# The scan's inputs u by channel ahead of group in one DMA, and the lag rows in one piece per partition, issued from ScalarE's queue

## The chip, the cores and the metric

One core of one Trainium2 chip runs the whole kernel in one launch. The metric is device time in microseconds, the median of three runs.

## The reference

One encoder layer on x of 2048 positions by 1024 channels, all float32:

```
n = rmsnorm(x);  proj = n @ w_in               # q, k, v and u, 512 columns each
att = diff_attention(q, k, v)                  # 4 heads, ALiBi
ssm = bi_s5_glu(u)                             # 32 groups of 16 channels, 64 complex states, both directions
h = x + [att, ssm] @ w_out
h = h + relu(rmsnorm(h) @ w1)^2 @ w2;  y = rmsnorm(h)
```

`bi_s5_glu` runs a linear recurrence x_t = a x_(t-1) + B u_t over the 2048 positions in each direction, reads out C x_t, adds a skip term d u_t, and gates the gelu of the sum.

## The kernel before

The kernel has four phases: the projection, attention, the scan with its gate (`phase_ssm`), and the output projection with the MLP. The change lies in the scan, with a small part in the projection.

**Layout of the scan.** The 2048 positions are NJ = 256 chunks of T = 8 steps. The 32 groups are worked off in NQU = 4 quarters of G = 8 groups; each group has GH = 16 channels. A step of the loop is one pair (group, direction), so a quarter has 16 steps and the phase NPAIR = 64. `u_t` holds the inputs of two quarters: partition (s, h), that is step in chunk and channel, and free dimensions group and chunk. `load_u` fills it for a quarter with eight DMAs, one for each s, each of 16 partitions by 8 groups in runs of 256 floats (1 KB), since `u_s` in HBM lies as (g h) s j.

**Within a chunk** an output depends on the inputs of the same chunk through a 128 by 128 matrix for each group, `toeplitz`, whose block (s, s') depends on the lag alone. TensorE computes the blocks of the 15 lags (`lags`, line 1923), ScalarE copies them to `strip` (16 partitions; `make_strip`, lines 1712 and 1713), GpSimd adds the two terms of the middle lag (`add_middle`, 1679 and 1681), and eight DMAs on the sync engine's queue (`load_toeplitz`, 1582) copy eight windows of `strip` to eight blocks of 16 partitions of `toeplitz`, in runs of 128 floats (512 B).

**A step on each engine.** TensorE: `inputs(n)`, two matmuls against `u_t` (1936, 1937); at i = 8 to 11 of a quarter four transposes of the next quarter's `bp` (`turn_b`, 1910); at i = 12 and 14 half of the next lags; and at each second step `outputs`, output number m = (step - 6)/2: the matmul with `toeplitz` (1947), then four with `cp` (1952). So the first output of quarter q, number 8q, is in TensorE's order behind step 16q + 6. VectorE: `turn_back` (1806), `add` (1812), `scan` (1820) and for the forward direction `turn_forward` (1567); GpSimd has the backward one. ScalarE: `gelu(m)` (1721), which then issues the store of its result to `z_s` (1723) on its own queue. TensorE may be no more than two steps ahead of `turn_back`, and every engine works in program order.

**The sync engine** issues everything else in a fixed order, group by group (n from 0 to 31): at the first group of a quarter `bp` and `cp` of the next (1358, 1371, 1373), at the second `load_u` of the next, at the seventh `load_toeplitz` of the next; for each group the table six groups ahead (`load_tab`, 512 KB, once both directions of group n are through) and the load of z of three groups back (`load_z`, once its store has landed). `load_toeplitz(0)` stands ahead of the loop and waits for GpSimd. At step 32 VectorE also splits the gate's weights (1851).

**Projection.** `split_w(i)` splits the i-th piece of 128 columns of `w_in` in a high and a low part on ScalarE (644) and VectorE (734); pieces 12 to 15 are those of u. `evacuate_qku` writes their results (759) and `store` stores them to `u_s` (547).

Of the kernel before, what the change touches and what calls it, by code (L numbers as in the profile page):

```python
# [17 lines left out]
F32 = mybir.dt.float32  # L18
# [375 lines left out]
def phase_project(nc, ctx, shared, x_t, norm1_g, w_in, qk_s, v_s, u_s, prep_in, attention_in):  # L394
# [110 lines left out]

    @block.sync
    def _(sp):
# [25 lines left out]
        def store(n):  # L533
# [197 lines left out]
    def _(dve):  # L731
        def split_w(i):
            dve.wait_ge(w_hi_ready, i + 1)
            dve.tensor_tensor(w_lo[:, :, w_slot(i)], w_raw[:, i % 2], w_hi[:, :, w_slot(i)].bitcast(F32),  # L734
# [602 lines left out]
class SsmHead:  # L1337
# [88 lines left out]
def phase_ssm(nc, ctx, place, shared, head, following, mag, s_d, w_glu, b_glu, z_s, ssm_s, att_s, att_square, att_floor,  # L1426
# [22 lines left out]
    strip = place.sb("sm_strip", 4096, [GH, G, 2 * T - 1, GH])  # L1449
# [4 lines left out]
    toeplitz = place.sb("sm_toeplitz", 38912, [P, 2, G, P])  # L1454
# [115 lines left out]
    def _(sp):  # L1570
# [6 lines left out]
        def load_toeplitz(q):  # L1577
            sp.wait_ge(strip_step, 4 * q + 4)
            if q >= 2:
                sp.wait_ge(y_done, (q - 1) * G)  # L1580
            for s in range(T):
                sp.dma_start(toeplitz[s * GH:(s + 1) * GH, q % 2].rearrange("p g (s h) -> p g s h", s=T),
                             strip[:, :, T - 1 - s:2 * T - 1 - s]).then_inc(toeplitz_loaded, 16)

# [13 lines left out]
        load_toeplitz(0)  # L1598
        for n in range(NGR):
            q, g = n // G, n % G  # L1600
            if q + 1 < NQU:
# [7 lines left out]
                if g == G - 2:  # L1609
                    load_toeplitz(q + 1)  # L1610
# [48 lines left out]
    def _(pool):  # L1659
# [14 lines left out]
        def add_middle(n):  # L1674
            q, half = n // 2, n % 2
            gs = slice(half * 4, half * 4 + 4)
            mid = strip[:, gs, T - 1]
# [16 lines left out]
    def _(act):  # L1694
# [10 lines left out]
        def make_strip(q, half):  # L1705
            n = 2 * q + half
            gs = slice(half * 4, half * 4 + 4)
            fwd, bwd = (lag_ps[0:GH, d].rearrange("p (g s h) -> p g s h", g=4, s=T) for d in range(2))
# [42 lines left out]
        for half in range(2):  # L1751
            make_strip(0, half)
# [1205 lines left out]
```

## Time and profile before

| | |
|---|---|
| median of 3 runs | 2610.61 us (2609.18 to 2612.34) |
| the profiled execution | 2613.55 us, its span 2611.6 us |
| TensorE, VectorE, ScalarE, GpSimd busy | 97%, 80%, 54%, 10% of the span |
| projection and attention | 0 to 958 us |
| scan, first transpose to last output | 959 to 1143.5 us |
| gate | 1143.5 to 1193 us |
| output projection and MLP | from 1193 us |

In a timeline a row has the start, the busy time, the engine and line, the operation and its tiles, the number merged, and in brackets the idle time before it and what ended it. In busy time by stretch, a row has the stretch and its length, then for each engine the busy time and number of instructions, then the granted clock (1.00 is 2.4 GHz, 0.50 is 1.2 GHz), the DMA share (mean busy share of the 16 DMA engines; it can exceed 1 where two queues' packets overlap) and GB/s. PEld is TensorE's weight load, SPq and ACTq are the queues of the sync engine and of ScalarE.

### The profile page before, as it was taken

How to read it: one execution, taken by the hardware profiler on the slowest of the kernel's cores; microseconds unless marked ns; L12 is line 12 of the kernel's file. 1: busy time of each engine (PE TensorE's matmuls, PEld its weight loads, DVE VectorE, ACT ScalarE, POOL GpSimd, SP SyncE). 2: the span in 40 equal slices, each digit the busy share in tenths (PEclk: the TensorE clock that was granted, in tenths of full speed). 3: DMA queues.
4: the chain of work that ended last, by engine and by line, in shares of the span. 5: the costliest groups of instructions: out<-in, count | busy, mean ns of one | idle time of the engine just before them, and what ended most of it. 6: DMA issues, size and time to landing. Idle time of an engine off the chain costs nothing.

```text
span 2611.6 us, 32904 instructions
## 1 busy us (share of the span) xinstructions
PE 2539.0 (97%) x12816; PEld 2077.5 (80%) x12816; DVE 2076.9 (80%) x2116; ACT 1416.9 (54%) x1754; POOL 269.7 (10%) x290
## 2 busy tenths in 40 slices
PE   9998999999999989899989999999999999999998
PEld 7887878878777867778767888888887888888886
DVE  5875759999999967879899777687789877678885
ACT  5276637778787752144435566533345666543334
POOL 3500022212121113310000000000000000000003
PEclk9999999999999999999999999999999999999999
DMA  6256642020204119946485543533334554452221
GB/s 213 111 189 230 235 123 64 25 72 23 72 25 104 32 60 265 265 164 221 182 313 216 210 181 136 224 145 129 123 114 162 220 220 177 177 195 97 97 79 65
DMA packets 158170, 388.78 MB, mean 149 GB/s; under 512 B 29120, under 2 KB 86720, under 8 KB 130240
## 3 DMA queue, kind: packets, MB, share of 16 engines
q1 hardware_dynamic: 142464, 319.58, 37.4%
q10 hardware_dynamic: 15552, 67.12, 6.5%
q8 instruction: 101, 1.65, 0.3%
q14 instruction: 53, 0.43, 0.1%
HBM read 266.58 MB, written 117.96 MB: 147 GB/s over the span
## 4 chain that ended last, share of the span: by engine, by line
PE 51%; DVE 4%; DMA 1%; issue 1%; ACT 0%; POOL 0%; SPq 0%; DVEq 0%; ACTq 0%; POOLq 0%
PE sm_banks L2799 16%; PE sm_banks L2801 16%; PE sm_banks L2800 16%; PE sm_banks L1997 1%; PE sm_banks L1995 1%; PE sm_banks L1996 1%; DVE ml_res L2657 1%; DMA kp_low<-hn_s 0%; DVE ml_b_split L2588 0%; DVE ml_w_split L2599 0%; DVE kp_tabs L2696 0%; DVE ml_hb L2704 0%; DVE ml_rinv L2683 0%; DVE ml_res L2677 0%; PE sm_banks L1952 0%
## 5 line engine op out<-in xcount | busy, mean ns | idle before, releaser
L2799 PE MATMUL sm_banks<-ml_b_split,ml_w_split 128*128 128x512 f32 x2016 | 788.8, 391 | 12.8 <-issue 10.7
L2800 PE MATMUL sm_banks<-ml_b_split,ml_w_split 128*128 128x512 f32 x2016 | 785.8, 390 | 0.0
L2801 PE MATMUL sm_banks<-ml_b_split,ml_w_split 128*128 128x512 f32 x2016 | 785.5, 390 | 0.0
L2799 PEld LDWEIGHTS sm_banks<-ml_b_split,ml_w_split 128*128 128x128 f32 x2016 | 379.6, 188 | 96.9 <-issue 15.6
L2800 PEld LDWEIGHTS sm_banks<-ml_b_split,ml_w_split 128*128 128x128 f32 x2016 | 379.7, 188 | 79.3 <-issue 1.0
L2801 PEld LDWEIGHTS sm_banks<-ml_b_split,ml_w_split 128*128 128x128 f32 x2016 | 379.4, 188 | 79.2
L1082 ACT ACTIVATE at_e<-at_e,at_neg_top 128x2048 f32<-128x2048 f32 x128 | 256.5, 2004 | 143.1 <-DVE at_neg_top L1136 143.1
L2425 ACT ACTIVATE ml_b_split<-kp_u_t 128x2048 fp32r<-128x2048 f32 x54 | 103.6, 1918 | 300.0 <-PE sm_banks L2801 296.4
L2657 DVE TENSOR_TENSOR ml_res<-sm_banks,ml_res 128x2048 f32<-128x2048 f32 x75 | 171.7, 2289 | 114.5 <-PE sm_banks L2801 114.5
L1238 PEld LDWEIGHTS pj_banks<-at_v,at_a_t 128*128 128x128 f32 x2048 | 238.4, 192 | 22.8 <-issue 22.6
L1238 PE MATMUL pj_banks<-at_v,at_a_t 128*128 128x128 f32 x2048 | 255.8, 278 | 0.0
L2588 DVE TENSOR_TENSOR ml_b_split<-kp_low,ml_b_split 128x2048 fp32r<-128x2048 f32 x53 | 121.3, 2288 | 96.5 <-ACT ml_b_split L2425 96.5
L1129 DVE CUSTOM_DVE_ANT_0 at_e<-pj_banks,at_bias,at_top 128x1024 f32<-128x1024 f32 x128 | 164.4, 1284 | 28.0 <-PE pj_banks L1210 25.5
L2425 ACT ACTIVATE ml_b_split<-kp_low 128x2048 fp32r<-128x2048 f32 x53 | 101.5, 1914 | 141.3 <-PE sm_banks L2801 136.0
L2396 POOL TENSOR_TENSOR kp_tabs<-kp_tabs,ml_square 128x512 f32<-128x512 f32 x13 | 22.8, 1750 | 1431.0 <-ACT ml_square L2491 1428.8
L1152 DVE SCALAR_TENSOR_TENSOR at_e<-at_e,at_coef 128x1024 f32<-128x1024 f32 x128 | 164.6, 1287 | 2.3
L1129 DVE CUSTOM_DVE_ANT_0 at_e<-pj_banks,at_bias 128x1024 f32<-128x1024 f32 x128 | 151.6, 1222 | 16.9 <-issue 15.4
L2588 DVE TENSOR_TENSOR ml_b_split<-kp_u_t,ml_b_split 128x2048 fp32r<-128x2048 f32 x54 | 123.4, 2286 | 52.3 <-ACT ml_b_split L2425 52.3
L858 PE MATMUL pj_banks<-pj_x_hi,pj_w_hi 128*128 128x512 f32 x384 | 152.5, 397 | 4.5 <-DVE pj_w_lo L734 4.5
L1205 PE MATMUL pj_banks<-at_k_hi,at_q_hl 128*128 128x512 f32 x512 | 151.7, 416 | 2.6 <-DVE at_top L1129 2.3
L859 PE MATMUL pj_banks<-pj_x_lo,pj_w_hi 128*128 128x512 f32 x384 | 150.3, 392 | 0.0
L860 PE MATMUL pj_banks<-pj_x_hi,pj_w_lo 128*128 128x512 f32 x384 | 150.2, 391 | 0.0
(246 smaller groups left out, 3994.5 us busy)
## 6 DMA issues: line engine op xcount, KB each, us to landing
act_s<-ml_res ACTq DMA_DIRECT2D x32, 1024.0 KB, 3.9
kp_wide<-in_w_stream SPq DMA_DIRECT2D x18, 1024.0 KB, 5.1
kp_tabs<-in_w_stream SPq DMA_DIRECT2D x18, 1024.0 KB, 7.1
kp_bp<-in_w_stream SPq DMA_DIRECT2D x18, 1024.0 KB, 5.5
ml_r<-in_w_stream SPq DMA_DIRECT2D x18, 1024.0 KB, 7.1
tab_s<-kp_tabs ACTq DMA_DIRECT2D x32, 512.0 KB, 2.8
kp_low<-hn_s SPq DMA_DIRECT2D x16, 1024.0 KB, 5.4
kp_u_t<-hn_s SPq DMA_DIRECT2D x16, 1024.0 KB, 4.9
```

Source lines behind the costliest of these rows:

```text
L858: pe.matmul(out, w_hi[:, k, cols], x_hi[:, k], start=(k == 0), stop=False)
L1082: act.activation(self.e[:, n % 2, c], self.e[:, n % 2, c], ACT.Exp, bias=self.neg_top[:, n % 2, c:c + 1], scale=self.SCALE, accum_out=self ...
L1129: dve.tensor_tensor_reduce(out=self.e[:, s % 2, c, half * self.HALF:(half + 1) * self.HALF], in0=self.score[:, c], in1=self.bias[:, at:at ...
L1152: dve.scalar_tensor_tensor(self.e[:, slot, 0, cols], self.e[:, slot, 1, cols], self.coef[:, 1:2], self.e[:, slot, 0, cols], ALU.mult, ALU. ...
L1205: pe.matmul(self.score[:, c, bank * TB:(bank + 1) * TB], self.q_hl[:, n % 2, c], self.k_hi[h % 2][:, c, keys], start=True, stop=False)
L1238: last = pe.matmul(self.pv[:, n % 2, 0:P], self.a_t[:, n % 2, kt], self.v[h % 2][kt], start=(kt == 0), stop=(kt == self.NQ - 1))
L2425: act.activation(b_split[g % 2][:, 0], raw_b(k, i)[:], ACT.Copy).then_inc(b_hi_ready, 1)
L2588: dve.tensor_tensor(b_split[g % 2][:, 1], raw_b(k, i)[:], b_split[g % 2][:, 0].bitcast(F32), ALU.subtract)\
L2657: dve.tensor_tensor(flat(res[reg]), flat(bank(k, i)), flat(res[reg]), ALU.add).then_inc(dve_left, 1)
L2799: pe.matmul(out, w_hi[:, w], b_hi[:, b], start=fresh and kt == 0, stop=False, skip_group_check=True)
L2800: pe.matmul(out, w_hi[:, w], b_lo[:, b], start=False, stop=False, skip_group_check=True)
L2801: last = pe.matmul(out, w_lo[:, w], b_hi[:, b], start=False, stop=kt == 3, skip_group_check=True)
```

## The change

`u_s` is laid out as [quarter, s, channel, chunk], and the channel dimension runs as (h g) where it ran as (g h). For that, the columns of the last four pieces of `w_in` are permuted while they are split: both splits read the raw piece with a stride of 16 floats and write in order. A quarter of u is then one DMA of 128 rows of 8 KB. `strip` is [16, lag, h, g], so that a window of eight lags is one run of 1024 floats (4 KB) per partition, and `toeplitz` holds the group as its last dimension; the matmul reads its weights with a stride of 8 floats (32 B). ScalarE's and GpSimd's writes to `strip` go in runs of four floats. The eight toeplitz DMAs go from the sync engine's program to ScalarE's: for quarter 0 behind `make_strip`, for the others in two halves, behind the gelu of step 16q and of step 16q + 2, that is behind gelu(8q - 3) and gelu(8q - 2).

```diff
     def load_u(self, sp, q):
-        for s in range(T):
-            sp.dma_start(self.u_t[s * GH:(s + 1) * GH, q % 2],
-                         self.u_s[q].rearrange("(g h) s j -> s h g j", g=G)[s]).then_inc(self.u_loaded, 16)
+        sp.dma_start(self.u_t[:, q % 2].rearrange("p g j -> p (g j)"),
+                     self.u_s[q].rearrange("s (h g) j -> (s h) (g j)", g=G)).then_inc(self.u_loaded, 16)
...
-    strip = place.sb("sm_strip", 4096, [GH, G, 2 * T - 1, GH])
+    strip = place.sb("sm_strip", 4096, [GH, 2 * T - 1, GH, G])
-    toeplitz = place.sb("sm_toeplitz", 38912, [P, 2, G, P])
+    toeplitz = place.sb("sm_toeplitz", 38912, [P, 2, P, G])
...
-        load_toeplitz(0)
         for n in range(NGR):
-                if g == G - 2:
-                    load_toeplitz(q + 1)
...
+        def load_toeplitz(q, first, end):
+            act.wait_ge(strip_step, 4 * q + 4)
+            if q >= 2:
+                act.wait_ge(y_done, (q - 1) * G)
+            for s in range(first, end):
+                act.dma_start(toeplitz[s * GH:(s + 1) * GH, q % 2].rearrange("p k g -> p (k g)"),
+                              strip[:, T - 1 - s:2 * T - 1 - s].rearrange("p s h g -> p (s h g)")).then_inc(toeplitz_loaded, 16)
...
+        load_toeplitz(0, 0, T)
         for step in range(NPAIR):
             if output_at(step) is not None:
                 gelu(output_at(step))
+            if q and i in (0, 2):
+                load_toeplitz(q, i * 2, i * 2 + 4)
...
-            pe.matmul(o, toeplitz[:, q % 2, g], u_t[:, q % 2, g], start=True, stop=False)
+            pe.matmul(o, toeplitz[:, q % 2, :, g], u_t[:, q % 2, g], start=True, stop=False)
...
-    u_s = scratch("u_s", [NQU, P, T, NJ])
+    u_s = scratch("u_s", [NQU, T, P, NJ])
```

## Rows read from the trace of the kernel before

**Rows 1.** Busy time by stretch, cut where the first output of a quarter starts

```profile
core 0: us, PE busy (x) PEld busy (x) DVE busy (x) ACT busy (x) POOL busy (x), PEclk, DMA share, GB/s
...
977.40:1017.70 40.30, 37.19 (x192) 31.59 (x193) 34.73 (x61) 10.71 (x23) 15.62 (x13) 1.00 1.07 273
1017.70:1065.80 48.10, 42.34 (x192) 34.90 (x193) 32.90 (x53) 8.79 (x22) 13.06 (x12) 0.89 1.04 262
1065.80:1109.40 43.60, 37.72 (x193) 31.23 (x192) 36.71 (x65) 8.56 (x22) 15.94 (x13) 0.96 1.07 264
1109.40:1143.50 34.10, 31.10 (x133) 25.98 (x134) 29.91 (x47) 7.23 (x14) 10.83 (x10) 0.89 0.49 136
```

**Rows 2.** Timeline of TensorE, 955 to 1146 us: pieces with idle time before them

```profile
977.47 0.67 PE L1947 MATMUL sm_banks<-kp_u_t,sm_toeplitz 128*128 128x256 f32 x2 [0.92 <-DMA sm_toeplitz<-sm_strip]
...
1017.72 1.19 PE L1947 MATMUL sm_banks<-kp_u_t,sm_toeplitz 128*128 128x256 f32 x2 [3.05 <-DMA sm_toeplitz<-sm_strip]
...
1026.51 0.66 PE L1910 MATMUL sm_banks<-sm_ident,kp_bp 128*128 128x128 f32 x4 [3.06 <-DMA kp_bp<-bp_s]
...
1055.64 1.22 PE L1936 MATMUL sm_banks<-kp_u_t,sm_p_t 128*128 128x256 f32 x2 [2.69 <-DVE sm_turned_w L1806]
...
1091.17 0.67 PE L1936 MATMUL sm_banks<-kp_u_t,sm_p_t 128*128 128x256 f32 x2 [0.78 <-DVE sm_turned_w L1806]
...
1109.42 1.19 PE L1947 MATMUL sm_banks<-kp_u_t,sm_toeplitz 128*128 128x256 f32 x2 [4.69 <-DMA sm_toeplitz<-sm_strip]
```

**Rows 3.** Timeline of VectorE, 1046 to 1116 us

```profile
1047.98 0.69 DVE L1806 TENSOR_TENSOR sm_turned_w<-sm_banks,kp_tabs 128x512 f32<-128x512 f32 x1 [2.72 <-DMA kp_tabs<-tab_s]
...
1051.62 3.36 DVE L1851 TENSOR_TENSOR sm_wg_lo<-sm_wg,sm_wg_hi 128x2048 fp32r<-128x2048 f32 x1
...
1114.56 0.69 DVE L1806 TENSOR_TENSOR sm_turned_w<-sm_banks,kp_tabs 128x512 f32<-128x512 f32 x1 [4.19 <-PE sm_banks L1937]
```

**Rows 4.** Timeline of the sync engine's queue, 955 to 1146 us: its DMA issues, merged

```profile
969.92 5.54 SPq L1582 DMA_DIRECT2D sm_toeplitz<-sm_strip  x8
...
1001.41 6.55 SPq L1582 DMA_DIRECT2D sm_toeplitz<-sm_strip  x8
...
1014.29 0.41 SPq L1358 DMA_DIRECT2D kp_bp<-bp_s  x1
...
1017.50 14.37 SPq L1362 DMA_DIRECT2D kp_u_t<-u_s  x8
...
1060.74 0.38 SPq L1358 DMA_DIRECT2D kp_bp<-bp_s  x1
```

**Rows 5.** Timeline of ScalarE: the issue of the seventh z store

```profile
1010.05 0.33 ACTq L1723 DMA_DIRECT2D z_s<-sm_z_g  x1
```

**Rows 6.** DMA issues, 955 to 1146 us: KB each, median us to landing

```profile
z_s<-sm_z_g ACTq DMA_DIRECT2D x32, 128.0 KB, 8.3
...
sm_toeplitz<-sm_strip SPq DMA_DIRECT2D x32, 64.0 KB, 9.3
```

**Rows 7.** The same view of 1117 to 1126 us, where DMA is lighter

```profile
z_s<-sm_z_g ACTq DMA_DIRECT2D x2, 128.0 KB, 3.9
```

**Rows 8.** Busy time in short stretches (columns as in rows 1)

```profile
971.00:977.00 6.00, 4.19 (x16) 2.41 (x14) 5.95 (x11) 0.00 (x0) 1.63 (x1) 1.00 0.62 97
979.50:984.00 4.50, 4.50 (x24) 3.98 (x23) 4.50 (x8) 1.26 (x3) 2.02 (x2) 1.00 1.07 395
992.50:996.50 4.00, 4.00 (x22) 3.36 (x20) 1.89 (x4) 1.50 (x4) 1.31 (x3) 1.00 1.14 136
1018.00:1021.40 3.40, 3.40 (x10) 2.72 (x10) 0.92 (x2) 0.00 (x0) 0.04 (x1) 0.56 1.10 254
```

**Rows 9.** Lines 1947, 756 and 759: ns min/median/max of one

```profile
L1947 PEld LDWEIGHTS sm_banks<-kp_u_t,sm_toeplitz x64: 186/190/337, 977.4 to 1140.8; 128*128 128x128 f32 x64
...
L756 DVE TENSOR_TENSOR pj_qku_out<-pj_banks,kp_bp x32: 681/692/694, 40.1 to 197.3; 128x512 f32<-128x512 f32 x32
...
L759 DVE TENSOR_TENSOR pj_qku_out<-pj_banks,kp_bp x16: 1078/1132/1147, 234.2 to 384.2; 128x512 f32<-128x512 f32 x16
```

More of the change, by code:

```diff
@@ L504, in w_slot, with w_raw_columns, w_split_columns @@
         return slice((i % HALF_W) * P, (i % HALF_W + 1) * P)
+    def w_raw_columns(i):
+        raw = w_raw[:, i % 2]
+        return raw if i < HALF_W + NV else raw.rearrange("p k (g h) -> p k h g", g=G)
+    def w_split_columns(w, i):
+        part = w[:, :, w_slot(i)]
+        return part if i < HALF_W + NV else part.rearrange("p k (h g) -> p k h g", g=G)
     @block.sync
@@ L733, in split_w @@
             dve.wait_ge(w_hi_ready, i + 1)
-            dve.tensor_tensor(w_lo[:, :, w_slot(i)], w_raw[:, i % 2], w_hi[:, :, w_slot(i)].bitcast(F32),
+            dve.tensor_tensor(w_split_columns(w_lo, i), w_raw_columns(i), w_split_columns(w_hi, i).bitcast(F32),
                               ALU.subtract).then_inc(w_lo_ready, 1)
@@ L1575, in load_cp @@
             head.load_cp(sp, q)
[L1577 to L1583, printed above, removed]
         def load_z(n):
@@ L1676, in add_middle @@
             gs = slice(half * 4, half * 4 + 4)
-            mid = strip[:, gs, T - 1]
+            mid = strip[:, T - 1, :, gs].rearrange("p h g -> p g h")
             pool.wait_ge(strip_copied, 3 * n + 3)
@@ L1707, in make_strip @@
             gs = slice(half * 4, half * 4 + 4)
-            fwd, bwd = (lag_ps[0:GH, d].rearrange("p (g s h) -> p g s h", g=4, s=T) for d in range(2))
+            fwd, bwd = (lag_ps[0:GH, d].rearrange("p (g s h) -> p s h g", g=4, s=T) for d in range(2))
             act.wait_ge(lag_done, n + 1)
             wait(act, toeplitz_loaded, 16 * T * q)
-            act.activation(strip[:, gs, T - 1:], fwd, ACT.Copy).then_inc(strip_copied, 1)
-            act.activation(strip[:, gs, 0:T - 1], bwd[:, :, 0:T - 1], ACT.Copy).then_inc(strip_copied, 1)
+            act.activation(strip[:, T - 1:, :, gs], fwd, ACT.Copy).then_inc(strip_copied, 1)
+            act.activation(strip[:, 0:T - 1, :, gs], bwd[:, 0:T - 1], ACT.Copy).then_inc(strip_copied, 1)
             wait(act, strip_step, 2 * n - 1)
-            act.activation(middle[:], bwd[:, :, T - 1], ACT.Copy).then_inc(strip_copied, 1)
+            act.activation(middle[:].rearrange("p g h -> p h g"), bwd[:, T - 1], ACT.Copy).then_inc(strip_copied, 1)
+        def load_toeplitz(q, first, end):
[5 more added lines that the diff above has]
+                              strip[:, T - 1 - s:2 * T - 1 - s].rearrange("p s h g -> p (s h g)")).then_inc(toeplitz_loaded, 16)
         def gelu(n):
```

7 lines of the change are left out of this document (4 added, 3 removed).

## The prediction

> **What bounds the kernel now.** I read first the page, by which TensorE is busy nearly throughout, then the busy time by stretch of the scan, cut at the first outputs (numbers 0, 8, 16, 24) of its four quarters. In the first, 40.3 us long, TensorE has 37.2 us of work at full clock, VectorE 34.7; the second takes 48.1 us and the third 43.6 for the same TensorE work, and the DMA share is over 1 in all three [rows 1]. So a quarter is worth 37.2 us to TensorE, and what lies above is stalls: 3.1, 10.9 and 6.4 us. The DMA engines are full, but only what TensorE waits for counts.
>
> The timeline of TensorE names the stalls: toeplitz not landed (0.92, 3.05, 4.69 us), `bp` not landed (3.06), VectorE late (2.69, 0.78) [rows 2]. Behind the 3.05 comes a stretch of 3.4 us at a granted clock near 0.5 [rows 8], the lower level of 1.2 GHz; it costs half its length, 1.65 us. The mean clock of 0.89 over 48.1 us [rows 1] is 5.3 us lost, or three such stretches, one for each long stall of that quarter (3.05, 3.06, 2.69).
>
> VectorE's timeline says what a stall is worth. The 2.69 stands behind the 3.36 us split of the gate's weights; VectorE had lost 2.72 us to a table a little earlier, but TensorE had not finished the next inputs much earlier: VectorE would have been at the split only about half a microsecond sooner, so without that wait most of the 2.69 remains. The 4.69 became 4.19 us of idle VectorE, which is not idle again by a TensorE stall up to the last scan [rows 3]: 4.2 us is its worth, clock included.
>
> The sync queue's timeline shows who is late: the toeplitz issues hold it 5.54 and 6.55 us, the next `bp` comes behind them, and eight issues of u take 14.37 us [rows 4].
>
> **What the change can give back**, in us of the profiled execution:
>
> - the toeplitz stalls: 0.9, then 3.05 + 1.65 of clock, then 4.2: 9.8
> - the `bp` stall: 3.06 + 1.65 = 4.7. `bp` was issued at 1014.29 and wanted at 1023.45 (1026.51 less 3.06) [rows 2, 4]. The 6.55 us of toeplitz issues no longer stand ahead of it, so it is issued 4 or 5 us sooner, behind less traffic. I count all of it.
> - the late tables: 0.5 of the 2.69 and the 0.78: 1.3
>
> Together 15.8.
>
> **u in one DMA.** While u lands the rate is 136 GB/s at a share of 1.14; with tables, `bp` and `cp` it is 395 at 1.07 [rows 8]. A quarter's 1.05 MB goes from 7.7 us of full engines to 2.7, and the sync queue's eight issues (14.37 us at worst) to one like that of `bp`, 0.53 or less [rows 4]. This is 5 of 40 us of DMA, and it makes the items above likely; it enters the sum only through them. Quarter 0's is loaded in attention, beside other work. The store of u has the same pieces of 256 B and is hidden in the projection: nothing.
>
> **Toeplitz by ScalarE.** What is removed from the sync queue is counted. What is added is the question when the last rows land. ScalarE issues at 0.33 us each, by the z store [rows 5], against some 0.6 to 2.5 on the sync queue; four hold it 1.3 us, and the next gelu is due only an output later, nine matmuls of 0.43 or 3.9 us: free. Even at 0.7 each it would be.
>
> The last four stand behind gelu(8q - 2) and its z store. In quarter 1 that store was issued at 1010.05, and TensorE asked for output 8 at 1014.67 (1017.72 less 3.05) [rows 2, 5]: 4.6 us. At quarter 0, with nothing beside them, the copies ran at 97 GB/s and a share of 0.62 [rows 8], though issues every 0.7 us may have set that. If 97 is the pace, 0.26 MB take 2.7 us; with 0.33 for the store's issue and about 1.8 us of latency (my estimate, from a z store in the light stretch at 3.9 us, less its own transfer and queue) the last rows land 4.8 us behind the z store's issue: a stall of 0.2 at best. At worst they land like a z store under load, 8.3 us behind an issue [rows 6], the last of which is 1.3 us late: 9.6, a stall of 5.0. `bp(q + 1)` is issued at just that time (1060.74 in quarter 2) [rows 4], so neither end is right; the burst of the quarter before has drained, and the z store in the lighter stretch took 3.9 [rows 7]. I take 2.0 for quarters 1 and 2, with half the price of a slow stretch (0.8), since stalls of 0.92 and 2.69 lie on either side of it: 2.8 each. Quarter 3 loads no `bp`, `cp` or u: 1.0.
>
> In quarter 0 the sync queue no longer waits for GpSimd and sends `bp` and `cp` (3.4 MB, 8.6 us at 395 GB/s) at about 968 instead of 975.5, just ahead of the toeplitz rows. Output 0 is asked for at 976.55. Eight issues end at 972.7 instead of 975.5, but at 97 GB/s they land at 977.2 alone and by about 982 behind the whole burst: a stall of 0.7 to 5; I take 2.0 and 0.8 of clock. The writes to `strip` in runs of four floats could add up to 1.2 us, at the ratio below, on this chain alone; that is within the bound. Later strips are copied a third of a quarter ahead.
>
> Toeplitz stalls after: 3 x 2.8 + 1.0 = 9.4.
>
> **The strided weights.** Of 64 weight loads of 190 ns each [rows 9] every one reads 128 floats with a stride of 32 B. They hide behind a matmul pass of 215 ns (two passes of a matmul of 256 columns are 0.43 apart in TensorE's steady state). No TensorE operand in this trace has such a stride. The nearest row is VectorE's line 759, the same tensor_tensor as line 756 but with operands read at a stride of 32 B: 1132 against 692 ns, 0.86 ns more for each of 512 elements [rows 9]. At that price a load takes 300 ns, 85 beyond the pass, and 64 of them 5.4 us. The other end is nothing, and a gain is excluded, as the hidden load can't get under the pass. Since line 759 also reads PSUM so, I take the middle, 2.7.
>
> On this the Trainium skill (SBUF — State Buffer, Door 1, the note on lines of 16 bytes) says that reads which go to a new line each time pay a penalty, so that four fp32 is as far as one strides free. Line 759 agrees; by that rule alone the 5.4 would stand in the sum.
>
> **The split of u's weights** reads with a stride of 64 B, four pieces on each of two engines: at most 0.9 us each, several groups ahead of TensorE's use. Nothing; without that cover, 3.5 us.
>
> **The sum.** 15.8 - 9.4 - 2.7 = 3.7 us. The profiled execution took 2613.55 us (span 2611.6); 2609.9 after. It lies 2.9 above the median shown, so the median becomes 2606.9. From the terms' ends near their values the forecast's own range is 2602 to 2611. A change of less than 0.2% (5.2 us) is about what a measurement of this kernel can't tell from none.
>
> **The rivals.**
>
> 1. *The relief is full.* The toeplitz rows land on time but for 0.7 to 1 us a quarter, and the weights cost nothing: 15.8 - 4 = 11.8, so 2598.8. For it: ScalarE's queue is short, the copies of 4 KB runs may be quicker than 97 GB/s. Against it: `bp` in the same microseconds.
> 2. *The strided weights set the pace.* At VectorE's price in full the gain is 15.8 - 9.4 - 5.4 = 1.0: 2609.6. At twice the load time (380 ns, 165 beyond the pass) it is a loss of 4.2: 2614.8. It would show as a longer TensorE quarter without stalls.
> 3. *The lag rows come later than before: slower.* The sync queue issued those of quarter 1 from 1001.41 to 1007.96 [rows 4], and ScalarE ends them about 3.5 us later; they land like a z store under load. Stalls: 5.0 + 1.65 in quarters 1 and 2, 5.0 in 3, about 5.1 in 0: 23.4 against 15.8 with free weights, so 7.6 slower, 2618. It decides from some 3 us a quarter. The rate is a reason for it: 16 source partitions may allow no more than the 97 GB/s seen, however long the runs.
> 4. *The change doesn't relieve anything that TensorE waits for*, the `bp` stall moving with the toeplitz one: 2610.6.
>
> The Trainium skill (SBUF — State Buffer, Door 1) ties a DMA's rate to how many of 16 ports its partitions reach, and 16 partitions in a row reach four. The 97 GB/s of rows 8 agrees, and it makes rival 3 likelier; u's eight DMAs were of that kind, so for u it speaks for the change.
>
> **Chances.** The forecast 0.38 (0.12 of it beyond 5.2 us faster, 0.26 within); rival 1 0.28; rival 2 0.10, half within and half slower; rival 3 0.17; rival 4 0.07. So faster 0.12 + 0.28 = 0.40, same 0.26 + 0.05 + 0.07 = 0.38, slower 0.05 + 0.17 = 0.22. The range runs from beyond the full relief (2595) to rival 3 (2618).
>
> **What the profile after would show.** u's issues one a quarter; the wait for `bp` at output 8 gone; the 2.69 still there behind line 1851; weight loads of line 1947 between 190 and 300 ns; waits for toeplitz of 1 to 3 us in each quarter, longest in 0 to 2; a DMA share near 0.95. The prediction is wrong if these waits are gone (faster) or over 3 us (slower), or if a stretch of a quarter without stalls is longer than 37.2 us.

## The result and the profile after

| | before | after |
|---|---|---|
| median | 2610.14 us (2609.18 to 2612.34) | 2636.86 us (2635.80 to 2638.40) |
| ratio | | 1.0089 [1.0077, 1.0101], slower |
| span of the profiled execution | 2611.6 us | 2634.6 us |
| scan's first inputs start | 967.9 | 971.3 |
| output 0, 8, 16, 24 start | 977.5, 1017.7, 1065.8, 1109.4 | 988.4, 1038.2, 1085.7, 1130.8 |

The forecast was 2606.9 us and its range ended at 2618. The change is slower by 23 us by the spans of the two profiled executions and by 27 by the medians. Where they come in, in the spans: 3.4 before the scan starts, 7.5 up to output 0, 9.6 in quarter 0 (49.8 us where it had 40.3), then -0.6, +1.5 and +0.3 in quarters 1 to 3, and 1.3 behind the scan.

Busy time by stretch of the kernel after, cut at the same outputs as [rows 1]:

```profile
core 0: us, PE busy (x) PEld busy (x) DVE busy (x) ACT busy (x) POOL busy (x), PEclk, DMA share, GB/s
971.20:988.40 17.20, 7.37 (x31) 4.89 (x29) 11.55 (x20) 2.45 (x4) 3.96 (x4) 0.86 0.95 269
988.40:1038.20 49.80, 40.61 (x192) 34.44 (x192) 33.46 (x56) 10.70 (x23) 14.55 (x12) 0.88 0.68 212
1038.20:1085.70 47.50, 41.56 (x193) 34.95 (x193) 36.35 (x57) 8.91 (x22) 14.53 (x12) 0.93 0.78 215
1085.70:1130.80 45.10, 39.71 (x193) 33.86 (x193) 34.88 (x59) 8.91 (x22) 14.53 (x12) 0.96 0.98 270
1130.80:1165.20 34.40, 31.63 (x131) 27.22 (x132) 30.09 (x46) 7.22 (x14) 10.97 (x10) 0.86 0.29 83
```

The DMA share is down from 1.07, 1.04 and 1.07 to 0.68, 0.78 and 0.98: u no longer fills the engines, as foreseen. The stretches are longer all the same. TensorE's timeline, pieces with idle time before them (it answers to [rows 2]):

```profile
988.36 1.22 PE L1957 MATMUL sm_banks<-kp_u_t,sm_toeplitz 128*128 128x256 f32 x2 [8.46 <-DMA sm_toeplitz<-sm_strip]
...
1038.25 1.22 PE L1957 MATMUL sm_banks<-kp_u_t,sm_toeplitz 128*128 128x256 f32 x2 [9.24 <-DMA sm_toeplitz<-sm_strip]
...
1071.38 0.70 PE L1946 MATMUL sm_banks<-kp_u_t,sm_p_t 128*128 128x256 f32 x2 [2.24 <-DVE sm_turned_w L1816]
...
1085.68 1.07 PE L1957 MATMUL sm_banks<-kp_u_t,sm_toeplitz 128*128 128x256 f32 x2 [3.65 <-DMA sm_toeplitz<-sm_strip]
...
1130.78 1.22 PE L1957 MATMUL sm_banks<-kp_u_t,sm_toeplitz 128*128 128x256 f32 x2 [5.39 <-DMA sm_toeplitz<-sm_strip]
```

The wait for `bp` is gone, though `bp` was not issued sooner: it left 36.5 us behind the start of output 0 (1024.84 less 988.36), before the change 36.8, and the 9.24 us for the lag rows now cover its landing. The 2.69 behind the split of the gate's weights is 2.24. And the waits for the lag rows are 8.46, 9.24, 3.65 and 5.39 us, 26.7 in all, where they were 0.92, 3.05, 0 and 4.69. Behind each of the four, TensorE works for a while at a granted clock of 0.50, the lower level:

```profile
988.40:993.80 5.40, 5.40 (x13) 4.30 (x14) 0.00 (x0) 0.38 (x1) 0.00 (x0) 0.50 0.64 262
1038.30:1041.60 3.30, 3.30 (x8) 2.70 (x9) 0.00 (x0) 0.00 (x0) 0.00 (x0) 0.50 1.00 225
1086.10:1089.40 3.30, 3.30 (x9) 2.64 (x9) 0.00 (x0) 0.00 (x0) 0.00 (x0) 0.50 1.09 317
1130.80:1133.70 2.90, 2.90 (x7) 2.37 (x8) 0.50 (x1) 0.00 (x0) 0.00 (x0) 0.50 1.04 275
```

These are 14.9 us of work that would take half as long at the upper level: 7.4 us lost.

The issues, first on the sync queue (answering to [rows 4]), then on ScalarE's (with [rows 5]):

```profile
971.35 0.32 SPq L1369 DMA_DIRECT2D kp_bp<-bp_s  x1
...
979.72 0.44 SPq L1372 DMA_DIRECT2D kp_u_t<-u_s  x1
...
1024.84 0.62 SPq L1369 DMA_DIRECT2D kp_bp<-bp_s  x1
...
1117.09 0.41 SPq L1594 DMA_DIRECT2D kp_bp<-att_s  x1
...
973.40 5.09 ACTq L1722 DMA_DIRECT2D sm_toeplitz<-sm_strip  x8
...
1024.94 0.33 ACTq L1730 DMA_DIRECT2D z_s<-sm_z_g  x1
1025.32 2.52 ACTq L1722 DMA_DIRECT2D sm_toeplitz<-sm_strip  x4
...
1077.26 2.45 ACTq L1722 DMA_DIRECT2D sm_toeplitz<-sm_strip  x4
...
1120.61 2.46 ACTq L1722 DMA_DIRECT2D sm_toeplitz<-sm_strip  x4
```

u is one issue of 0.44 us. The eight copies of quarter 0 are issued right behind `bp` and `cp` and take ScalarE 5.09 us, 0.63 each and not 0.33. In quarter 1, the second four leave at 1025.32 to 1027.84, `bp` at 1024.84; TensorE asks for the rows at 1029.01 (1038.25 less 9.24) and has them 10.4 us behind the last issue. In quarter 3 the sync queue has a load that the prediction left out: 1 MB of attention's result (line 1594, into the tile of `bp`, which is free by then), issued at 1117.09, 3.5 us ahead of the last four copies. Landings, as in [rows 6]:

```profile
kp_tabs<-tab_s SPq DMA_DIRECT2D x15, 512.0 KB, 5.0
...
z_s<-sm_z_g ACTq DMA_DIRECT2D x32, 128.0 KB, 4.7
...
sm_toeplitz<-sm_strip ACTq DMA_DIRECT2D x32, 64.0 KB, 7.1
```

A z store lands in 4.7 us where it took 8.3. The copies of 4 KB runs on the emptier engines take 7.1 where those of 512 B took 9.3. Line 1957, the matmul with the strided weights, and its load (as [rows 9]):

```profile
L1957 PEld LDWEIGHTS sm_banks<-kp_u_t,sm_toeplitz x64: 312/333/342, 988.3 to 1162.1; 128*128 128x128 f32 x64
L1957 PE MATMUL sm_banks<-kp_u_t,sm_toeplitz x64: 397/403/791, 988.4 to 1162.5; 128*128 128x256 f32 x64
```

The load takes 333 ns for 190, the matmul 403 for 379. And the 3.4 us ahead of the scan are lost in one place, where TensorE waits for the split of a block of x. TensorE's timeline of before, then of after:

```profile
244.83 0.77 PE L853 MATMUL pj_banks<-pj_w_hi,pj_x_hi 128*128 128x512 f32 x1 [8.21 <-DVE pj_x_lo L741]
```

```profile
247.83 0.77 PE L864 MATMUL pj_banks<-pj_w_hi,pj_x_hi 128*128 128x512 f32 x1 [11.29 <-DVE pj_x_lo L752]
```

The first of the four splits of u's weight pieces in the kernel after, its high part on ScalarE and its low part on VectorE (the other three are alike; pieces of other columns take 1.06 and 1.22 us):

```profile
183.64 2.01 ACT L655 ACTIVATE pj_w_hi<-kp_wide 128x1024 fp32r<-128x1024 f32 x1 [2.75 <-DMA kp_wide<-in_w_in]
...
185.68 1.98 DVE L745 TENSOR_TENSOR pj_w_lo<-kp_wide,pj_w_hi 128x1024 fp32r<-128x1024 f32 x1 [2.81 <-ACT pj_w_hi L655]
```

### The profile page after: what moved, and what is told of

Its sections match the earlier page's. It is cut to its first block, busy times and chain, and to the rows that moved or that the text cites. A ratio compares the mean times of both kernels' runs of the same rounds, so it can differ in the third digit from the quotient of the medians.

```text
span 2634.6 us, 32878 instructions
## 1 busy us (share of the span) xinstructions
PE 2545.7 (97%) x12816; PEld 2085.4 (79%) x12816; DVE 2082.2 (79%) x2116; ACT 1420.7 (54%) x1754; POOL 271.1 (10%) x290
## 4 chain that ended last, share of the span: by engine, by line
PE 50%; DVE 4%; DMA 1%; issue 1%; ACT 0%; POOL 0%; SPq 0%; DVEq 0%; ACTq 0%; POOLq 0%
PE sm_banks L2809 16%; PE sm_banks L2811 16%; PE sm_banks L2810 16%; PE sm_banks L2007 1%; PE sm_banks L2005 1%; PE sm_banks L2006 1%; DVE ml_res L2667 1%; DMA kp_low<-hn_s 0%; DVE ml_b_split L2598 0%; DVE ml_w_split L2609 0%; DVE kp_tabs L2706 0%; DVE ml_hb L2714 0%; DVE ml_rinv L2693 0%; PE sm_banks L1962 0%; DVE ml_res L2687 0%
## 5 line engine op out<-in xcount | busy, mean ns | idle before, releaser
L2809 PE MATMUL sm_banks<-ml_b_split,ml_w_split 128*128 128x512 f32 x2016 | 788.9, 391 | 12.6 <-issue 10.4
```

Source lines behind the costliest of these rows:

```text
L2809: pe.matmul(out, w_hi[:, w], b_hi[:, b], start=fresh and kt == 0, stop=False, skip_group_check=True)
```

## The experiments

All were timed in three sets, each beside the kernel before, and ratios are to it, with their 95% intervals. Its median was 2614.66 us in the first set (the four kernels with parts of the change), 2612.73 in the second (`early_issue`, `bp_behind`, `sp_contig`, `sp_write_strided`) and 2614.05 in the third (`sp_late`, `early_bp`, `sp_plain_split`, `sp_outer_later`). So times of different sets are compared by their ratios; a difference of two ratios is taken times 2610 us, and one below 0.15% can't be told from none.

### Which part costs: four kernels with parts of the change

**`u_alone`** has u's layout, its one DMA and the permuted columns; the lag rows are as before.

> Only u's part of the change: the layout of u_s, the permuted split of its weights, one DMA a quarter. The queue theory (what was lost comes from when and where the toeplitz copies are issued): nothing of the 23 us is here, and the relief that the prediction counted on is: the wait for bp at output 8 gone, 3 to 10 us faster than before, 2600 to 2607. The projection theory (the stride-16 reads of the split delay the projection by the 3.4 us by which the first inputs of the scan start later after the change): the scan starts 3.4 us later again and the sum is 0 to 3 us slower, 2610 to 2613.

Measured: 2607.60 us, 0.9973 [0.9963, 0.9983]. The waits for the lag rows fall to one of 0.87 us, with the old 512 B layout, because they land in 3.8 us (9.3 before):

```profile
984.07 0.75 PE L1955 MATMUL sm_banks<-kp_u_t,sm_toeplitz 128*128 128x256 f32 x2 [0.87 <-DMA sm_toeplitz<-sm_strip]
...
sm_toeplitz<-sm_strip SPq DMA_DIRECT2D x32, 64.0 KB, 3.8
```

Both theories hold in part: the relief came, 7 us by the ratio, and the scan starts at 974.5, 6.6 us later than before, with a wait of 13.69 us for the split of x.

**`layout_alone`** has the new `strip` and `toeplitz`, issued by the sync engine as before; u in eight DMAs.

> Only the layout of the lag rows (strip by lag, h, g; toeplitz with the group last; strided weights), copied from the sync engine's queue at the old places; u as before. The queue theory: toeplitz waits stay near those of before (0.9, 3.1, 0, 4.7 us), weight loads of 333 ns cost 0.05 to 0.14 us an output, 2 to 5 us in all: 2612 to 2615. The layout theory (copies in runs of 4 KB are themselves slower and later, weights cost most of the loss): 12 to 20 us slower, 2622 to 2630.

Measured: 2609.87 us, 0.9984 [0.9975, 0.9992]. Waits of 0.65, 1.80 and 3.92 us are left of 0.92, 3.05 and 4.69. Neither theory foresaw a gain; the new layout is a small one by itself, 0.16%, strided weights included.

**`queue_alone`** has the old layouts, and only `load_toeplitz` moved to ScalarE.

> Only the move: the eight copies of a quarter in the old layout (512 B runs) issued by ScalarE at the places of the change. The queue theory: the long toeplitz waits of the changed kernel appear again (8.5 at output 0, 9 at output 8, 4 to 5 at the others), 15 to 20 us slower than before: 2625 to 2630. The layout theory: waits within 2 us of those of before, at most 3 us slower: 2610 to 2613.

Measured: 2654.58 us, 1.0151 [1.0137, 1.0164], worse than the whole change and far beyond the 2625 to 2630 of the queue theory. The waits for the lag rows are 16.20, 16.61, 13.36 and 9.13 us; TensorE's timeline at the first, then the copies of quarter 0 alone:

```profile
991.86 1.19 PE L1947 MATMUL sm_banks<-kp_u_t,sm_toeplitz 128*128 128x256 f32 x2 [16.20 <-DMA sm_toeplitz<-sm_strip]
...
sm_toeplitz<-sm_strip ACTq DMA_DIRECT2D x8, 64.0 KB, 11.2
```

**`after_sp`** is the whole change but for the queue: the sync engine issues the rows at the old places.

```diff
+        load_toeplitz(0)
...
+                if g == G - 2:
+                    load_toeplitz(q + 1)
...
-        load_toeplitz(0, 0, T)
...
-            if q and i in (0, 2):
-                load_toeplitz(q, i * 2, i * 2 + 4)
```

> The whole change but the move: one DMA for u and the new lag layout, toeplitz copies by the sync engine at the old places. The queue theory: the waits at outputs 0 and 8 fall back under 2 us, 2602 to 2612, that is 25 to 35 us under the changed kernel. The layout theory: it stays within 8 us of the changed kernel, 2628 to 2637.

Measured: 2606.74 us, 0.9970 [0.9959, 0.9980]. Only 0.47 and 0.56 us of waits for the rows are left:

```profile
979.54 0.82 PE L1955 MATMUL sm_banks<-kp_u_t,sm_toeplitz 128*128 128x256 f32 x2 [0.47 <-DMA sm_toeplitz<-sm_strip]
...
1097.58 0.82 PE L1955 MATMUL sm_banks<-kp_u_t,sm_toeplitz 128*128 128x256 f32 x2 [0.56 <-DMA sm_toeplitz<-sm_strip]
...
sm_toeplitz<-sm_strip SPq DMA_DIRECT2D x32, 64.0 KB, 5.8
```

So the move to ScalarE's program costs 1.0089 less 0.9970, 1.2% or 31 us, and all else together gains 0.3%. That is the queue theory.

### Late, or in the wrong company?

Two things changed with the move: the rows of quarters 1 to 3 are issued later (quarter 1's from 1020.25 to 1027.84, of a scan that started 3.4 us later, against 1001.41 to 1007.96), and they run beside the sync queue's large loads (`bp` and `cp`, in quarter 3 the 1 MB of attention's result) and not ahead of them.

**`early_issue`**, on the kernel after, issues them one step before the quarter:

```diff
-            if q and i in (0, 2):
-                load_toeplitz(q, i * 2, i * 2 + 4)
+            if q + 1 < NQU and i == 15:
+                load_toeplitz(q + 1, 0, T)
```

> The kernel after, with all eight copies of a quarter's lag rows issued by ScalarE at step 15 of the quarter before (behind the last turned copy and the strip) and not four at step 0 and four at step 2 of the quarter itself. In the kernel after the rows landed 9.24, 3.65 and 5.39 us too late in quarters 1 to 3. Theory A (they are late because they are issued late): the first four now leave about 2 us sooner and the last four about 6 to 7 us sooner, so the waits of quarters 1 to 3 fall from 18.3 us in all to under 4, and the time falls by 12 to 17 us, to a ratio of about 1.003. Theory B (they are late because bp, cp and u, issued at the start of a quarter, share the DMA engines with them): the rows gain only what is moved before the burst starts; the waits fall to some 9 to 12 us, the time by 5 to 8 us, ratio about 1.006. The wait of quarter 0, 8.46 us, is the same by both.

Measured: 2616.77 us, 1.0017 [1.0008, 1.0027], 19 us faster than the kernel after. The waits of quarters 1 and 2 are gone and quarter 3's is 0.32; that of quarter 0 is as it was:

```profile
989.69 1.22 PE L1957 MATMUL sm_banks<-kp_u_t,sm_toeplitz 128*128 128x256 f32 x2 [8.52 <-DMA sm_toeplitz<-sm_strip]
```

Theory A, beyond its own estimate: a few microseconds sooner are enough for quarters 1 to 3. They are not enough to tell company from lateness, since the earlier rows also run ahead of `bp`.

**`bp_behind`**, on the kernel after, holds `bp` and `cp` back until the rows have landed:

```diff
                 if g == 0:
+                    sp.wait_ge(toeplitz_loaded, 16 * T * (q + 1))
                     sp.wait_ge(lag_done, 2 * q + 2)
```

> The kernel after, with one wait more on the sync engine: bp and cp of the next quarter are issued only when this quarter's lag rows have landed. Theory B (the rows share the engines with bp and cp): the eight copies of quarter 0 land as in a quiet stretch, about 3 to 4 us behind the last issue at 978.5 instead of 986.8, so the wait of 8.46 falls to 3 or 4 us, and the others from 9.24, 3.65 and 5.39 to 2 to 4 us each; together 10 to 15 us faster than the kernel after. What it may cost is a late bp, cp or table (up to 3 us). Theory A (they are late because ScalarE issues them late and slowly, 0.63 us each): the waits stay within 1 us of what they were, and the time is that of the kernel after or longer, ratio 1.009 or more.

Measured: 2618.84 us, 1.0027 [1.0013, 1.0040], 16 us faster than the kernel after. TensorE's waits, with the rows issued by ScalarE as in the kernel after, at the same distance from TensorE's need:

```profile
979.90 0.82 PE L1958 MATMUL sm_banks<-kp_u_t,sm_toeplitz 128*128 128x256 f32 x2 [0.52 <-DMA sm_toeplitz<-sm_strip]
...
1020.76 0.82 PE L1958 MATMUL sm_banks<-kp_u_t,sm_toeplitz 128*128 128x256 f32 x2 [2.17 <-DMA sm_toeplitz<-sm_strip]
...
1066.34 0.82 PE L1958 MATMUL sm_banks<-kp_u_t,sm_toeplitz 128*128 128x256 f32 x2 [1.89 <-DMA sm_toeplitz<-sm_strip]
...
1110.60 1.21 PE L1958 MATMUL sm_banks<-kp_u_t,sm_toeplitz 128*128 128x256 f32 x2 [5.57 <-DMA sm_toeplitz<-sm_strip]
```

Landing of the eight copies of quarter 0, here and in the kernel after:

```profile
sm_toeplitz<-sm_strip ACTq DMA_DIRECT2D x8, 64.0 KB, 2.4
```

```profile
sm_toeplitz<-sm_strip ACTq DMA_DIRECT2D x8, 64.0 KB, 8.6
```

Theory B, and again more than it asked: 2.4 us for 8.6, and a wait of 0.52 for 8.46. The packets of the trace show the company. In the kernel after, the 128 packets of 4 KB of quarter 0's rows start between 977.2 and 986.8 us, and 223 packets of the sync queue start between them, 179 of `cp` and 44 of a table (those of `bp` started from 972.3 to 975.5, so the first of the rows started 3.8 us behind its issue); in four equal parts of that time it is 36, 30, 28 and 33 of the rows beside 63, 47, 49 and 64 of the others. With `bp` behind, no other starts between them and they start 1.2 us behind their issue and are through in 4.9 us, which is the pace of ScalarE's issues (eight by 0.63 us). In `queue_alone` the same bytes are 1024 packets of 512 B, and they take 17.0 us beside 1110 others.

Quarter 3 keeps its wait. It isn't a later issue that sets it apart: in quarters 2 and 3 of both kernels the last issue ends 2.3 us before TensorE asks. With that same lead `bp_behind` waits 1.89 us in quarter 2, where its copies land in 4.8 us (median), and 5.57 in quarter 3, where they land in 7.8. What stands beside them there, and `bp_behind` does not hold back, is the 1 MB of attention's result, issued 3.5 us ahead of the last four as in the kernel after. No run holds back that load alone, so its share is argued and not shown.

On this the Trainium skill (DMA: Bandwidth & Descriptors, Queues, rings and completion order) says that a DMA engine takes the queues in turn and works off a whole packet of some 9 to 17 descriptors of one before it goes to the next. That would fit with small copies that wait for several rows of `cp` each time. The rows of the trace don't say which engine moved them, so the length of a turn isn't shown here.

**`sp_late`** tells the two apart the other way round: the sync engine's queue, with `bp` behind the rows, but in quarters 1 to 3 issued at the start of the quarter. Against `after_sp`:

```diff
+            if q and g == 0:
+                load_toeplitz(q)
             if q + 1 < NQU:
                 if g == 0:
...
-                if g == G - 2:
-                    load_toeplitz(q + 1)
```

> The kernel of the run after_sp, but the sync engine issues the lag rows of quarters 1 to 3 only at the start of the quarter itself, just ahead of bp and cp, at about the time at which ScalarE does in the kernel after. Theory A (the time of issue decides): they come too late as in the kernel after, by about 3 to 8 us in each of quarters 1 to 3, a ratio of 1.004 to 1.008. Theory B (ScalarE's queue decides, because its packets take turns with those of the sync engine's queue while bp and cp stand behind the rows on the sync engine's own): the waits are 1 to 3 us each as in bp_behind, 0.52, 2.17 and 1.89 there in the first three quarters, and the ratio is 1.000 or less.

Measured: 2622.86 us, 1.0036 [1.0022, 1.0049].

```profile
1021.24 1.22 PE L1955 MATMUL sm_banks<-kp_u_t,sm_toeplitz 128*128 128x256 f32 x2 [3.68 <-DMA sm_toeplitz<-sm_strip]
...
1068.44 1.22 PE L1955 MATMUL sm_banks<-kp_u_t,sm_toeplitz 128*128 128x256 f32 x2 [4.18 <-DMA sm_toeplitz<-sm_strip]
...
1114.33 1.22 PE L1955 MATMUL sm_banks<-kp_u_t,sm_toeplitz 128*128 128x256 f32 x2 [5.10 <-DMA sm_toeplitz<-sm_strip]
...
sm_toeplitz<-sm_strip SPq DMA_DIRECT2D x32, 64.0 KB, 3.5
```

Each copy lands in 3.5 us, the quickest of all these kernels, and still they come 3.7 to 5.1 us too late. But they were issued later than was meant: in quarters 1 to 3 the last issue ends 1.8, 2.0 and 1.2 us behind TensorE's asking (1017.56 in quarter 1), where in the kernel after it ends 1.2, 2.3 and 2.3 us ahead of it. So these waits show what lateness can do and are not its share in the kernel after. Theory A is nearer, but neither is whole: late issue costs 0.66% over `after_sp` (17 us), and the kernel after another 0.53% (14 us), by its waits in quarters 0 and 1 (8.46 and 9.24 us, here 0.46 and 3.68), where its rows run beside `cp`, in quarter 1 beside `bp` too.

**`early_bp`** puts both remedies on the kernel after: `early_issue`, and `bp` behind the rows in quarter 0 alone.

> The kernel of the run early_issue (ScalarE issues a quarter's eight copies at step 15 of the quarter before; 1.0017 of before), and in quarter 0 alone the sync engine holds bp and cp back until the lag rows have landed, as in bp_behind, where the wait of quarter 0 was 0.52 us instead of 8.5. If the loss of the change is made of these two things, issued late in quarters 1 to 3 and behind bp and cp in quarter 0, both together take it away: waits for the lag rows of under 2 us in all, 7 to 9 us faster than early_issue, ratio about 0.9985 to 0.997, that of after_sp. If ScalarE's queue costs something of its own beside that, the ratio stays over 1.000.

Measured: 2607.07 us, 0.9979 [0.9969, 0.9989], where `after_sp` has 0.9970. Waits of 0.56 and 0.32 us for the rows are left (and in quarter 1 of 1.76 for `bp` and 1.44 for `cp`):

```profile
980.80 0.82 PE L1959 MATMUL sm_banks<-kp_u_t,sm_toeplitz 128*128 128x256 f32 x2 [0.56 <-DMA sm_toeplitz<-sm_strip]
...
1103.07 0.82 PE L1959 MATMUL sm_banks<-kp_u_t,sm_toeplitz 128*128 128x256 f32 x2 [0.32 <-DMA sm_toeplitz<-sm_strip]
```

ScalarE's queue by itself costs nothing that these runs can tell. The time of issue and the large loads beside it are the whole loss. They overlap: in quarter 1 either remedy alone takes most of the wait away (9.24 us to 0 by issuing earlier, to 2.17 by holding `bp` back).

### The strides

**`sp_contig`**, on top of `after_sp`:

```diff
-            pe.matmul(o, toeplitz[:, q % 2, :, g], u_t[:, q % 2, g], start=True, stop=False)
+            pe.matmul(o, toeplitz[:, q % 2].rearrange("p k g -> p (k g)")[:, g * P:(g + 1) * P], u_t[:, q % 2, g], start=True, stop=False)
```

> The kernel of the run after_sp (the whole change, but the lag rows issued by the sync engine at their old places), with the weights of each output's first matmul read as 128 floats in a row and not with a stride of 32 B. It multiplies the rows of other groups, so the output isn't the reference's; the work is the same in count and size. Theory A (the strided loads, 333 ns each, are hidden but for 0.05 to 0.14 us per output): 2 to 4 us faster than after_sp, ratio about 0.996; the loads take 190 ns again. Theory B (they are hidden altogether, since TensorE waits for VectorE's tables and scans anyway): the same as after_sp within 1 us, ratio 0.997. At VectorE's price in full, as in rival 2, it would be 5.4 us.

Measured: 2603.74 us, 0.9969 [0.9959, 0.9979], against 0.9970 for `after_sp`: no difference that can be told. The matmul is back at 379 ns:

```profile
L1955 PE MATMUL sm_banks<-kp_u_t,sm_toeplitz x64: 379/379/634, 983.8 to 1135.6; 128*128 128x256 f32 x64
```

By TensorE's timeline the stride does cost something. An output with nothing else behind it takes 3.89 us here (1009.18 to 1013.07) and 3.93 in `after_sp`; with the next quarter's transposes or lags behind it the stride adds 0.14 or 0.15, as 4.77 (988.21 to 992.98) against 4.91 (984.09 to 989.00). From output 1 to output 8, with no wait between, it is 32.63 against 33.34 us. With five of the dearer sort in each of quarters 0 to 2, the 32 outputs come to 2.9 us (an estimate from these rows), 0.11%, which the intervals can't tell from nothing: theory A as well as B fits the ratio, and the rows speak for A.

**`sp_plain_split`**, on top of `after_sp`:

```diff
-        return raw if i < HALF_W + NV else raw.rearrange("p k (g h) -> p k h g", g=G)
+        return raw
...
-        return part if i < HALF_W + NV else part.rearrange("p k (h g) -> p k h g", g=G)
+        return part
```

> The kernel of the run after_sp, with u's weight pieces split in their own order, read and written in a row as before the change. The channels of u are then not permuted, so the output isn't the reference's; the work is the same in count and size. Theory A (the strided splits are the cause of TensorE's longer wait for the x split at 236 us, 10.7 to 14.6 us in the five kernels with u's part against 7.7 to 8.6 in the three without): the splits take 1.06 and 1.22 us, the wait is 7.7 to 8.6 us again, and the kernel is 3 to 5 us faster than after_sp, ratio 0.9955. Theory B (it is something else, the order of tables and stores or the clock): the wait stays over 10.5 us, ratio 0.997.

Measured: 2601.33 us, 0.9954 [0.9941, 0.9966], the fastest of all. The wait for the split of x, in `after_sp` and here:

```profile
246.91 0.76 PE L862 MATMUL pj_banks<-pj_w_hi,pj_x_hi 128*128 128x512 f32 x1 [10.28 <-DVE pj_x_lo L750]
```

```profile
243.71 0.76 PE L862 MATMUL pj_banks<-pj_w_hi,pj_x_hi 128*128 128x512 f32 x1 [7.56 <-DVE pj_x_lo L750]
```

2.7 us of it are gone, the scan starts at 967.0 for 970.4, and the ratio says 0.16% or 4 us, with intervals that overlap. The other kernels bear it out: in the nine that split u's weights with a stride (and leave the coefficients where they were) the wait is 10.28 to 14.25 us and the scan starts at 970.4 to 974.6; in the four without it is 7.34 to 8.21 and 967.0 to 967.9. So the cause is shown. Its size is not sharp: `after_sp` and `sp_contig` have the same projection, and theirs are 10.28 and 14.25.

**`sp_write_strided`**, on top of `after_sp`, asks whether the other side of the split is cheaper:

```diff
-        return raw if i < HALF_W + NV else raw.rearrange("p k (g h) -> p k h g", g=G)
+        return raw if i < HALF_W + NV else raw.rearrange("p k (g h) -> p k g h", g=G)
...
-        return part if i < HALF_W + NV else part.rearrange("p k (h g) -> p k h g", g=G)
+        return part if i < HALF_W + NV else part.rearrange("p k (h g) -> p k g h", g=G)
```

> The kernel of the run after_sp, with the permutation of u's four weight pieces done by the other side of the split: the raw weights are read in a row and the parts are written with a stride of 32 B, where the change reads with a stride of 64 B and writes in a row. In all kernels with u's part those splits took 2.0 us each on ScalarE and 2.0 on VectorE, against 1.06 and 1.22 before, and TensorE waited 3 to 5 us longer for the x split at 236 us. Theory A (the reads are what a stride makes dear): ScalarE's four splits are back to about 1.06 us, VectorE's, which read one operand strided still, to 1.2 to 1.6, and most of the 3 us come back: 2 to 3 us faster than after_sp. Theory B (a stride costs the same on either side): 2.0 us each again, and the time of after_sp, ratio 0.997.

Measured: 2607.40 us, 0.9985 [0.9976, 0.9994]. Theory B, and a little worse: the splits take 2.16 us on ScalarE, not 1.06, and the kernel is 0.15% slower than `after_sp`, at the edge of what can be told.

```profile
184.17 2.16 ACT L653 ACTIVATE pj_w_hi<-kp_wide 128x1024 fp32r<-128x1024 f32 x1 [2.51 <-DMA kp_wide<-in_w_in]
```

The Trainium skill (SBUF — State Buffer, Door 1, the note on lines of 16 bytes) tells of a penalty for each access that goes to a new line; writes with a stride of 32 B pay here as reads with one of 64 B do, 2.16 and 2.00 us.

**`sp_outer_later`**, on top of `after_sp`, moves one block of VectorE's coefficients from group 35 to 39, behind the split of x:

```diff
-PREP_OUTERS = (26, 29, 32, 35, 41, 44, 49, 52)
+PREP_OUTERS = (26, 29, 32, 39, 41, 44, 49, 52)
```

> The kernel of the run after_sp, with one block of coefficients (three VectorE products of 2.55 us each, at 228.8 to 236.3 in that run) made four groups later, behind the split of x that TensorE waits for at 236. Theory A (the cover of the strided splits is gone because VectorE and ScalarE are behind with the coefficients and the tables, so that all that is added there reaches TensorE): the wait of 10.7 us falls by 5 to 8 us, and the kernel is 5 to 9 us faster than after_sp, ratio about 0.994. Theory B (the x split waits for x itself, or for the buffers): the wait stays over 9 us and the time within 2 us of after_sp.

Measured: 2615.50 us, 1.0008 [0.9999, 1.0016], 10 us slower than `after_sp`. The first wait falls by 3.4 us to 6.88, less than theory A said, and a wait of 8.58 us comes in at the next block of x:

```profile
298.56 0.77 PE L862 MATMUL pj_banks<-pj_w_hi,pj_x_hi 128*128 128x512 f32 x1 [8.58 <-DVE pj_x_lo L750]
```

Neither theory: the block does stand in the way at 236, but moved it costs more than it gives, and the scan starts at 979.0. What is left of the first wait is ScalarE's. The split of x begins with its high part there, and ScalarE comes to that only behind its tables: in this kernel it is at them from 226.5 us on without a pause of over 0.5 us, and in `after_sp` it also waits 3.25 us for VectorE, which is at the coefficients. Its start, in `after_sp` and here:

```profile
245.25 5.02 ACT L664 ACTIVATE pj_x_hi<-kp_low,pj_gain 128x512 fp32r<-128x512 f32 x8 [0.46 <-ACT kp_tabs L376]
```

```profile
241.68 5.01 ACT L664 ACTIVATE pj_x_hi<-kp_low,pj_gain 128x512 fp32r<-128x512 f32 x8 [0.46 <-ACT kp_tabs L376]
```

In `sp_plain_split` it starts at 242.06, 3.2 us sooner than in `after_sp`: that is the way by which the strided splits, about 1 us more on ScalarE for each of four, reach TensorE.

## Why the prediction was wrong

**The failed step** is the landing of the lag rows, put at 2.0 us of stall and 0.8 of clock each for quarters 0 to 2 and 1.0 for quarter 3, together 9.4. Measured are waits of 8.46, 9.24, 3.65 and 5.39, together 26.7, and 7.4 for the lower clock. Three parts of the step were wrong.

- *The issue.* I priced it by the z store, 0.33 us. The copies took 0.61 to 0.64 each on ScalarE, 5.09 for eight; on the sync engine of `after_sp` 5.01 for eight. The nearer row was in my hands: [rows 4] has eight in 5.54, or 0.69 each, and I read that as a slow queue. It also explains the 97 GB/s of [rows 8]: 64 KB each 0.69 us are 95 GB/s, so that was the pace of issue. The rows of quarter 0 in `bp_behind`, alone and issued each 0.63 us, went at 106 GB/s (0.52 MB in 4.9 us), so neither 16 partitions nor the length of the runs held them to 97; whether 16 partitions would hold them to something higher no run here shows.
- *The company.* I put `bp(q + 1)` in the worst case and took a value near the lower end, as "the burst of the quarter before has drained". The new burst decides, in quarter 0 that of `cp`. In quarter 1 the rows were there 13.3 us behind the issue of the z store (1038.25 less 1024.94), where I had 4.8 at best and 9.6 at worst. `bp_behind` shows it: with nothing else changed, 8.46, 9.24 and 3.65 become 0.52, 2.17 and 1.89. For quarter 3 I named `bp`, `cp` and u, none of which it loads, and took 1.0; it was 5.39, and 5.57 in `bp_behind`, with the 1 MB of attention's result beside the rows.
- *The reserve.* In quarter 1 the old issues began 13.3 us ahead of TensorE's need (1014.67) and ended 6.7 ahead; the new ones began 8.8 ahead of it and ended 1.2 ahead. I priced the 3.5 us by which the last of them would be later, lost 5.5, and counted the rest of the lead as free. `early_issue` gives the lead back: 9.24, 3.65 and 5.39 become 0, 0 and 0.32, since the rows are then both earlier and ahead of the loads.

**What the stalls cost** besides: 7.4 us for the lower clock, where I had counted 0.8 behind each of three, 2.4.

**Rival 3** is what happened, with its mechanism and place, at 23.4 us of stalls. Its size was off, 7.6 us slower where 23 to 27 were measured, because its price per quarter was bounded by a z store's landing; and its second reason, a rate of 97 GB/s from 16 partitions, is not what happened. It had a chance of 0.17, and the range of the prediction ended at its 2618.

**The relief of 15.8 us** came, as far as these runs can tell. `u_alone` shows that u in one DMA takes away the waits for the rows, but for 0.87 us, and that for `bp` (a wait of 2.21 for `cp` comes in at 1038.59). In `after_sp` the waits for rows, `bp` and `cp` are 1.7 us in all, and the 2.69 stayed, at 2.24. Its span is 11.1 us below that of before, and 15.8 less 1.0 for rows, 2.5 for the later start (970.4 for 967.9) and 2.9 for the strided weights are 9.4. The ratio says 0.30%, 5 to 11 us; the profiled execution of `after_sp` (2602.24) is 4.5 us below that kernel's median, so the nearness of the two spans is not proof to the microsecond. The way was not the one that I gave: `bp` was to be issued 4 or 5 us sooner because the rows leave the sync queue. It left 36.8 us behind output 0's start before, 36.5 in the kernel after, but 34.8 in `u_alone`, 35.0 in `layout_alone` and 33.9 in `after_sp`, and in these three the rows are still in that queue. So it was not their leaving it that brought `bp` sooner.

**The split of u's weights** was put at nothing, and at 3.5 us without its cover. The price was right (0.95 us more on ScalarE and 0.77 on VectorE, four each) and the cover was not there. I looked at when TensorE needs those weights, and not at what else stands behind the splits on the same two engines: tables, coefficients, and at 236 us the split of x for which TensorE already waited 8.21 us in the kernel before. The scan starts 3.4 us later after the change, and `sp_plain_split` starts it 3.4 sooner than `after_sp`.

**The strided weights**: 2.7 us, from a load of 300 ns. The load is dearer (333), and the cost by the profile is 0.04 to 0.15 us an output, an estimated 2.9 in all; by the ratio it can't be told from nothing. The size was right. It was the middle between two ends, so that is luck: 85 ns beyond the pass for each load would be 5.4 us, 118 ns (333 less 215) 7.6, and less than half of that is left, so most of the long load is hidden.

**The longer runs in `strip`** on GpSimd and ScalarE showed nowhere beyond the bound.

**The sum.** I had 3.7 us faster, and the spans are 23.0 slower: 26.7 between them. The waits and their clock are 34.1 where I had 9.4, 24.7 more; the splits are 3.4 for nothing; the weights 2.9 for 2.7. Together 28.3, 1.6 more than the spans show. By the medians the forecast is off by 30.0 (2636.86 less 2606.9), since the profiled execution of before was 3.4 us above its median. Single executions of one kernel differ by some microseconds, so the sum is closed to about 3 us and no better; within that no term of weight is missing.

## What to carry to other kernels

A DMA that is issued early is worth its lead, not its issue time: before moving one, subtract the new issue time from the time of need, and put the whole burst issued next to it on another queue ahead of its last packet. When an edit makes an instruction dearer, its cover is what stands behind it on its own engine, down to the next thing that a waiting engine wants, not the slack of its own result. Of this change keep u in one DMA, and leave the lag rows on the sync queue, ahead of `bp`: `u_alone`, 0.9973. The new layout of the rows, worth 0.16% by itself, adds nothing to it that can be told: `after_sp` has 0.9970.

## What was unexpected in the hardware

- Copies of 64 KB from 16 partitions to 16 take 0.61 to 0.64 us to issue on ScalarE in 4 KB runs and 0.65 to 0.68 in 512 B runs, 0.59 to 0.63 on the sync engine in 4 KB runs where nothing holds them up; a z store of 128 KB from 128 partitions takes 0.33 on ScalarE.
- The landing of a small copy on one queue hangs on a large one on the other: 0.52 MB of rows took 9.6 us beside 1.8 MB of the sync queue's, 4.9 alone, and 17.0 in pieces of 512 B beside 3.0 MB.
- A split of 1024 floats per partition takes 1.06 us on ScalarE in order, 2.00 read with a stride of 64 B, and 2.16 written with one of 32 B; VectorE's 1.22 becomes 2.0 and 2.2.
- Weights with a stride of 32 B load in 333 ns for 190 and lengthen the matmul's record from 379 to 403 ns, but the time from one output to the next only from 3.89 to 3.93 us, and by 0.14 or 0.15 us where transposes or lags stand between.
